# Weight buffers at the upper end of the persistent on-chip memory

## The reference

```
for layer in range(2):
    h = rmsnorm(x, mix_norm[layer])
    x = x + (nsa_pool_mixer(h, ...) if layer % 2 == 0 else conformer_conv(h, ...))
    h = rmsnorm(x, ffn_norm[layer])
    x = x + swiglu(h, ffn_w_gate[layer], ffn_w_up[layer], ffn_w_down[layer])
# second block: gated linear attention and a short convolution, then a feed-forward, then a gate
h = h + concat([gla, y]) @ w_out
a, bb = split(u2 @ w_gate_upffn)
h = h + (silu(a) * bb) @ w_down
h = h + sigmoid(u3 @ w_ple_gate) * (p @ w_ple_proj)
```

## The kernel before

| tensor | before | after | after - before |
|---|---|---|---|
| raw | 16,512 | 89,536 | +73,024 |
| whi | 32,896 | 105,920 | +73,024 |
| wlo | 49,280 | 122,304 | +73,024 |
| x | 65,664 | 16,512 | -49,152 |
| act_hi | 82,048 | 32,896 | -49,152 |
| act_lo | 98,432 | 49,280 | -49,152 |
| rstd to wtap (small ones and t1, t2, t3) | 114,816 to 138,680 | 65,664 to 89,528 | -49,152 |
| hid_hi, hid_lo | 138,688, 163,264 | the same | 0 |
| bt_hi, bt_lo | 187,840, 200,128 | the same | 0 |
| sw_hi, sw_lo, ssum | 212,416, 218,560, 224,704 | the same | 0 |

## Time and profile before

### The profile page before, as it was taken

The page is one execution under the profiler, slowest core; times in us unless marked ns, Lnnn a source line. Parts: engine busy times, 40 slices in busy tenths (PEclk is TensorE's granted clock), DMA queues, the critical chain, the costliest instruction groups (busy, mean ns, idle before and its releaser), DMA issues.

```text
span 1789.1 us, 27531 instructions
## 1 busy us (share of the span) xinstructions
PE 1734.1 (97%) x10662; PEld 1498.1 (84%) x10662; DVE 1251.9 (70%) x1756; ACT 867.4 (48%) x1310; POOL 516.9 (29%) x356
## 2 busy tenths in 40 slices
PE   8999999999999999899999999999999999999997
PEld 6777788988998866689988998788788998899876
DVE  8667677754785798688744776678857875477575
ACT  5337556732773322456732763443335673277342
POOL 1342115502540246225502540012301550254000
PEclk9798999999999999899999999999999999999998
DMA  6210133333333465223333332422212333333332
GB/s 214 82 47 1 62 81 95 95 107 106 95 91 98 120 153 145 74 80 95 99 103 106 95 103 87 123 72 71 71 64 78 95 95 106 106 95 94 107 93 72
DMA packets 284699, 169.01 MB, mean 94 GB/s; under 512 B 8288, under 2 KB 278528, under 8 KB 284576
## 3 DMA queue, kind: packets, MB, share of 16 engines
q1 hardware_dynamic: 283664, 165.10, 32.7%
q0 software_dynamic: 624, 1.67, 0.3%
q10 hardware_dynamic: 288, 0.54, 0.1%
HBM read 156.59 MB, written 2.10 MB: 89 GB/s over the span
## 4 chain that ended last, share of the span: by engine, by line
PE 47%; DVE 6%; issue 1%; ACT 1%; POOL 0%; DVEq 0%; POOLq 0%; ACTq 0%
PE ps L1342 21%; PE ps L1027 8%; PE ps L1028 8%; PE ps L1029 8%; DVE wlo L1646 1%; DVE rstd L1688 1%; PE ps L1535 0%; ACT whi L602 0%; DVE act_lo L1678 0%; DVE act_lo L1676 0%; DVE wlo L1959 0%; DVE tt L1975 0%; DVE x L2439 0%; DVE bt_lo L1676 0%; DVE at L2305 0%
## 5 line engine op out<-in xcount | busy, mean ns | idle before, releaser
L1027 PE MATMUL ps<-act_hi,whi 128*128 128x512 f32 x796 | 320.0, 402 | 16.9 <-DVE act_lo L1678 8.8
L1028 PE MATMUL ps<-act_lo,whi 128*128 128x512 f32 x796 | 313.8, 394 | 0.0
L1029 PE MATMUL ps<-act_hi,wlo 128*128 128x512 f32 x796 | 313.0, 393 | 0.0
L602 ACT ACTIVATE whi<-raw 128x2048 fp32r<-128x2048 f32 (+3 forms) x104 | 167.0, 1606 | 233.7 <-PE ps L1029 219.4
L1646 DVE TENSOR_TENSOR wlo<-raw,whi 128x2048 fp32r<-128x2048 f32 (+3 forms) x96 | 191.3, 1993 | 42.7 <-ACT whi L602 42.5
L1342 PE MATMUL ps<-act_hi,whi 128*128 128x256 f32 x720 | 205.5, 285 | 11.2 <-ACT ps L773 6.9
L1027 PE MATMUL ps<-hid_hi,whi 128*128 128x512 f32 x528 | 209.8, 397 | 0.0
L1028 PE MATMUL ps<-hid_lo,whi 128*128 128x512 f32 x528 | 209.8, 397 | 0.0
L1029 PE MATMUL ps<-hid_hi,wlo 128*128 128x512 f32 x528 | 209.8, 397 | 0.0
L444 POOL TENSOR_TENSOR raw<-raw 128x512 f32<-128x512 f32 x60 | 82.3, 1372 | 437.5 <-DVE sqacc L1666 178.4
L1342 PE MATMUL ps<-act_hi,wlo 128*128 128x256 f32 x720 | 204.1, 283 | 0.0
(11 more groups left out here) (402 smaller groups left out, 3921.8 us busy)
## 6 DMA issues: line engine op xcount, KB each, us to landing
raw<-in_ffn_w_gate_dram SPq DMA_DIRECT2D x44, 512.0 KB, 3.9
raw<-in_ffn_w_up_dram SPq DMA_DIRECT2D x44, 512.0 KB, 5.1
raw<-in_w_gate_upffn_dram SPq DMA_DIRECT2D x44, 512.0 KB, 4.8
raw<-in_ffn_w_down_dram SPq DMA_DIRECT2D x32, 384.0 KB, 4.1
raw<-in_conv_w_pw_dram SPq DMA_DIRECT2D x24, 512.0 KB, 5.6
raw<-in_w_in_dram SPq DMA_DIRECT2D x24, 512.0 KB, 4.6
raw<-in_ffn_w_down_dram SPq DMA_DIRECT2D x32, 320.0 KB, 3.6
z<-z SPq DMA_DIRECT2D x28, 262.0 KB, 4.9
```

The source lines that it names most:

```text
L602: act.activation(whi[:, n % 2, 0:cols], raw[:, n % 2, 0:cols], ACT.Copy).then_inc(hi_done, 1)
L1027: pe.matmul(out, lhs[0], rhs[0], start=start, stop=False)
L1028: pe.matmul(out, lhs[0], rhs[1], start=False, stop=False)
L1029: return pe.matmul(out, lhs[1], rhs[0], start=False, stop=stop)
```

## The change

The three declarations of the weight buffers stand behind `wtap`, the last persistent tensor, and not ahead of `x`, the first. Nothing else is different. The instructions stand on every engine in the same order, with the same operands by name, the same shapes and the same waits; what differs is addresses, by the table above. The region's start is where it was.

```
-        raw = sb("raw", [P, 2, SLOT])
-        whi = sb("whi", [P, 2, SLOT], F32R)
-        wlo = sb("wlo", [P, 2, SLOT], F32R)
         x = sb("x", [P, KD, S])
         act_hi = sb("act_hi", [P, KD, S], F32R)
         act_lo = sb("act_lo", [P, KD, S], F32R)
...
         t3 = sb("t3", [P, 2, S])
         wtap = sb("wtap", [P, 2, CONV])
+        raw = sb("raw", [P, 2, SLOT])
+        whi = sb("whi", [P, 2, SLOT], F32R)
+        wlo = sb("wlo", [P, 2, SLOT], F32R)
```

## The result

The changed kernel takes 1776.62 us (median of 8 runs, 1772.17 to 1778.38) and the one before 1785.04 us (median of 8, 1780.78 to 1790.84; the three runs shown ahead of the prediction are among them). The ratio is 0.995 with a 95% interval of 0.994 to 0.996: 8.4 us faster, where 27 were forecast and 1746 to 1783 was the range. The time lies in the range, but the gain is under a third of the forecast. The range reached up to 1783 to take in a rival, the dear price at 512 columns, so that the time lies in it speaks for the rival and not for the forecast.

The account below looks back on a forecast made before the run. The prediction took TensorE, busy 97% of the span, as the bound. Its terms -10.8, -10.5 and -7.9, with 2 us given back as hidden, summed to -27 us: 1760 from a median of 1786.9, range 1746 to 1783.

Parts of the forecast that it names:

- What bounds the kernel: Whole kernel: TensorE is the limit, busy 97% of the span, so a nanosecond per matmul counts thousands of times.
- What the surcharge goes with: All matmul chains: time beyond one column per cycle goes with the weights-to-moving-operand distance modulo 512 bytes, not a buffer's place.
- (a): Gate and up panels, 60: act with whi/wlo at 256 columns gets cheaper, -10.8 us; bt with whi/wlo saves nothing.
- (b): Down panels: 1584 matmuls of hid with whi/wlo at 512 columns go from 233.3 to 226.7 ns, -10.5 us.
- (c): Projections, convolution, mixers, first panels, last gate: 2388 act with whi/wlo matmuls at 512 columns get 3.3 ns cheaper, -7.9 us.
- (d): Where (c) lies, TensorE partly waits, so some of the gain becomes idle time: 2 us off the sum.
- (e): Other engines: GpSimd's additions and DMA into raw at new addresses, at most +1.4 us on ScalarE's landing waits, taken as 0.
- the 512 column pair goes dear: Rival: act with whi/wlo at 512 columns takes hid's surcharge of 20.0 ns, +16.0 us, sum -5 (1782); chance 0.08.
- Nothing moves: Rival: the TensorE spacings come from something other than addresses, such as bank written or other engines; 1787 us, chance 0.12.
- Slower: Rival: place counts; whi and wlo border on hid's region and every pair with them pays 20.0 ns; +30 us (1817), chance 0.05.

Follow-up runs that it names:

- the later sweep: Three one-run kernels, the one before or the changed one with eps6 or eps5 moved and/or 64 or 96 unused bytes ahead of hid_hi: 1791.24, 1796.50 and 1790.61 us.
- the second experiment: The changed kernel with eps6, eps5 and wtap declared ahead of x, so act starts 320 bytes higher: 1782.43 us, ratio 0.9986 to the kernel before.
- the fourth experiment: The kernel before with eps6 and eps5 declared ahead of raw, weights and act both 64 bytes higher: 1783.00 us in one run.

## Why the prediction was wrong, by its own steps

**What bounds the kernel: right.** TensorE's sums account for 8.8 us and the median shows 8.4. In the gate and up stage TensorE is busy for 84.64 of the 85 us and no other engine limits. (The prediction gives the granted clock of 1.00 for all its timelines from rows that cover only the down stage's; the profile before has 1.00 from 820 to 908 and from 750 to 785 us too.)

**What the surcharge goes with: right in kind.** The distance of the two operands sets the price, not the place; the runs with 192 unused bytes and with the other order show it. Two corrections: it counts modulo 256, and at 256 columns it isn't the distance alone but also the chain ahead. Neither touched this change, whose act with whi/wlo chains are entered as those of act with sw were.

**(a): right.** -10.8 forecast, 262.6 to 251.9 us measured, -10.7. bt with whi/wlo was put at 0 and its mean rose by 0.4 ns, while its sum fell by 0.8 us.

**(b): right.** 226.7 ns forecast and measured. -10.5 by the price; -9.9 by the sums, which hold the waits.

**(c): the step that failed.** For act with whi/wlo at 512 columns -7.9 us was taken, 3.3 ns less each; it came out at +6.0 ns each, 2388 x 6.0 = +14.3 us by the price, +12.8 by the sums, and both lie outside the bounds of -15.5 and -3.1 that it had been given. The text said that no row had this pair of distance and size, and then bounded it by the row that shared the distance (256 columns, 192) and left the row that shared the size (512 columns, hid, 20.0 ns) to a rival with 0.08. But only two rows had the size, one at 0 and cheap, one not at 0 and dear; the reading that only 0 is cheap at 512 columns stood there, and the later sweep shows just that for all seven other steps of 32. That one distance has 11.6 and 20.0 at the two sizes was even written down, as something that the reading did not explain: it should have said that prices do not carry from one size to the other.

**(d), (e): small.** The 2 us that were to be hidden have no counterpart, since there was no gain at 512 columns to hide. GpSimd's additions took 1623 ns and not 1632, ScalarE's waits for landings 14.7 us and not 14.0.

For raw's new start (192 and not 128 bytes past a multiple of 256) the sum took 0, and the waits bear that out: the second and the fourth experiment, with the start at 192 too, have 14.1 and 14.4 us. But the start does show in the transfers themselves, by the queue that loads the weights (packets, MB, share of 16 engines' span), before and after:

```profile
q1 hardware_dynamic: 283664, 165.10, 32.7%
```

```profile
q1 hardware_dynamic: 283664, 165.10, 33.5%
```

32.7% of 1789.1 us is 585 us per engine, 33.5% of 1773.4 is 594. Over all runs it is 585 to 589 us with the start at 128 and 594 to 596 at 192, some 1% more. The estimate from "DMA: Bandwidth & Descriptors" ("How a descriptor splits into AXI transactions") in the Trainium skill was up to a tenth per load. The page speaks of what a transaction fetches, and here only the end that is written moved. The ScalarE group whose waits are meant, in the changed kernel:

```profile
L602 ACT ACTIVATE whi<-raw 128x2048 fp32r<-128x2048 f32 x48 | 91.5, 1906 | 112.2 <-PE ps L1029 97.5 <-DMA raw<-in_nsa_w_in_dram 11.1 <-DMA raw<-in_conv_w_pw_dram 3.6
```

With (c) at +14.3, and (d) left out, the prediction's own sum is -10.8 - 10.5 + 14.3 = -7.0, against -8.4 measured. The rival "the 512 column pair goes dear" (-5 us, chance 0.08) is what happened.

**The other rivals.** "Nothing moves" is refuted: 192 unused bytes change 1584 matmuls by 6.6 ns each. With it falls what the prediction drew from "TensorE: Matmul & The Clock Gate" ("Step-by-step: what each phase is for") in the Trainium skill, that addresses can't matter. The page says that loading the next weights doesn't steal read bandwidth from the running matmul; whether that itself is wrong, and by which path the two streams meet, no run shows. "Slower", the theory of the place, is refuted by the second experiment.

## What to carry to other kernels

Where TensorE is the limit with float32r operands and each matmul has weights of its own, look at the distance from start to start of one form by operand pair; if it differs, compute the operands' distance modulo 256 bytes from the addresses and move one by unused bytes. Here 512 column matmuls want 0 and the best for 256 columns has to be tried as a whole, since the price of a chain depends on the one ahead. And when a price has to be carried to a case without a row, a row of the same size and another distance may be nearer than one of the same distance and another size: let the bounds take in both unless a third row tells.

## What the runs showed that I had not expected

- The surcharge of a matmul beyond one column per cycle is 13.4 ns at best and about 20 ns otherwise at 512 columns (19.4 to 20.9 by distance); in cycles at 2.4 GHz (0.417 ns) 226.7 and 233.3 are 544 and 560, 32 and 48 over 512. At 256 columns 120.0 and 113.3 are 288 and 272, 32 and 16 over 256. What takes these 16 cycles is open.
- One distance has two lasting spacings, 113.5 and 117.7 ns, by what ran ahead.
- In the changed kernel VectorE's split of a gate and up panel takes 2505 ns in the mean and not 2356, and its busy time from 280 to 365 us rose from 66.37 to 70.76. The addresses are not needed to explain it: splits during which GpSimd adds nothing take 2286 ns in the mean before and 2289 after (at most 2294 in both). Those that run while GpSimd adds a quarter to ssum (L452) are the long ones, and there are 35 of them in 60 and not 19. The traces show that the two go together; no run parts cause from effect. It cost nothing, since TensorE ends last there. The group in the changed kernel:

```profile
L1959 DVE TENSOR_TENSOR wlo<-raw,whi 128x2048 fp32r<-128x2048 f32 x60 | 150.3, 2505 | 16.9 <-ACT whi L749 15.7
```
